# A hybrid decoder step: the sample stage's first loads in another order and on another queue

## The reference

```python
def mixer_block(h, pos, past, w_in, b_gate, w_conv, b_conv, mh_norm_g, w_out):
    proj = jnp.einsum('btd,dc->btc', h, w_in)              # q, k, v | raw q/k, v, o, gates of the mLSTM
    ...
    att = dilated_attention_sample(qa, kc, vc)             # 3 patterns: window 128 / 512 step 4 / 2048 step 16
    ...
    hb, C1, n1, m1 = mlstm_chunkwise(qb, kb, vb, ig, lf, C0, n0, m0, chunk)
    hb = hb * lax.rsqrt(jnp.mean(hb * hb, axis=-1, keepdims=True) + EPS)
    hb = hb * mh_norm_g.reshape(MLSTM_HEADS, MLSTM_HD)
    hb = hb * jax.nn.sigmoid(ob.reshape(B, T, MLSTM_HEADS, MLSTM_HD))
    mix = jnp.concatenate([att.reshape(B, T, ATT_WIDTH), hb.reshape(B, T, MLSTM_WIDTH)], axis=-1)
    return jnp.einsum('btc,cd->btd', mix, w_out), ...

hp = hp + a_p; hs = hs + a_s
hp = hp + sqrelu_mlp(rms_norm(hp, norm2_g), w_up, w_down)  # same for hs, then a last rms_norm
```

## Time and profile before

| | before |
|---|---|
| median of 3 runs | 2995.48 us (2992.3 to 2998.82) |
| the profiled execution | 2989.5 us, its span 2987.7 us |
| busy share of the span: TensorE, weight loads, VectorE, ScalarE, POOL | 96, 83, 48, 31, 34% |
| mean granted TensorE clock | 0.984 |

### The profile page before, as it was taken

One profiled execution on the slowest core, in us unless ns is written; L12 is line 12 of the kernel. 1 busy time (PEld: TensorE's weight loads), 2 busy tenths in 40 slices (PEclk: granted clock), 3 DMA queues, 4 the chain that ended last, 5 costly groups with the idle time before them and its releaser, 6 DMA issues.

```text
span 2987.7 us, 47542 instructions
## 1 busy us (share of the span) xinstructions
PE 2855.3 (96%) x18291; PEld 2478.0 (83%) x18291; DVE 1427.7 (48%) x3363; ACT 926.2 (31%) x1741; POOL 1003.3 (34%) x590
## 2 busy tenths in 40 slices
PE   7999999998999968899999999999999999999997
PEld 5878788887777756678799999989999998899996
DVE  5522555334888845586343333344333333544444
ACT  4301322112767742332132221243212222422222
POOL 1212012211455530210064343444434344545443
PEclk8999999999999988999999999999999999999999
DMA  4322223334464448955352323235222323533332
GB/s 137 113 102 97 97 94 122 106 117 147 133 193 155 160 141 335 370 174 187 134 220 94 126 93 107 94 122 225 94 108 93 126 93 117 207 129 131 138 126 83
DMA packets 124794, 421.41 MB, mean 141 GB/s; under 512 B 18655, under 2 KB 44387, under 8 KB 104918
## 3 DMA queue, kind: packets, MB, share of 16 engines
q1 hardware_dynamic: 103836, 366.53, 34.7%
q10 hardware_dynamic: 19658, 48.68, 4.2%
q0 software_dynamic: 1152, 4.19, 0.5%
HBM read 350.83 MB, written 135.63 MB: 163 GB/s over the span
## 4 chain that ended last, share of the span: by engine, by line
PE 48%; ACT 1%; POOL 1%; DVE 0%; DMA 0%; issue 0%; ACTq 0%
PE mlp_bank L220 16%; PE mlp_bank L221 16%; PE mlp_bank L222 16%; PE mlp_bank L236 0%; PE mlp_bank L235 0%; POOL mlp_wu_lo L2634 0%; DMA mlp_xb<-x 0%; PE mlp_bank L2982 0%; DVE mlp_acc L2854 0%; POOL mlp_xb L2676 0%; ACT mlp_wu_hi L2692 0%; ACT mlp_acc L2767 0%; DVE mlp_hT_lo L2903 0%; DVE mlp_acc L2871 0%; POOL mlp_acc L2681 0%
## 5 line engine op out<-in xcount | busy, mean ns | idle before, releaser
L2854 DVE TENSOR_TENSOR mlp_acc<-mlp_acc,mlp_bank 128x512 f32<-128x512 f32 x542 | 348.2, 684 | 365.7 <-PE mlp_bank L222 357.6
L220 PE MATMUL mlp_bank<-mlp_hT_hi,mlp_wu_hi 128*128 128x384 f32 (+1 forms) x1536 | 496.0, 323 | 3.1 <-PEq L3122 3.1
L222 PE MATMUL mlp_bank<-mlp_hT_hi,mlp_wu_lo 128*128 128x384 f32 (+1 forms) x1536 | 494.6, 322 | 0.0
L221 PE MATMUL mlp_bank<-mlp_hT_lo,mlp_wu_hi 128*128 128x384 f32 (+1 forms) x1536 | 494.4, 322 | 0.0
L2842 DVE TENSOR_TENSOR mlp_xn<-mlp_xn 128x384 f32<-128x384 f32 (+1 forms) x192 | 203.8, 1068 | 509.5 <-ACT mlp_xn L2710 489.3
L220 PE MATMUL mlp_bank<-mlp_wd_hi,mlp_u_hi 128*128 128x512 f32 x1024 | 400.0, 391 | 5.0 <-DVE mlp_acc L2854 5.0
L221 PE MATMUL mlp_bank<-mlp_wd_lo,mlp_u_hi 128*128 128x512 f32 x1024 | 398.9, 390 | 0.0
L222 PE MATMUL mlp_bank<-mlp_wd_hi,mlp_u_lo 128*128 128x512 f32 x1024 | 398.8, 389 | 0.0
L2638 POOL TENSOR_TENSOR mlp_wd_lo<-mlp_wd_raw,mlp_wd_hi 128x2048 fp32r<-128x2048 f32 x48 | 221.8, 4621 | 391.6 <-ACT mlp_wd_hi L2698 391.6
L2647 POOL TENSOR_TENSOR mlp_u_lo<-mlp_xn,mlp_u_hi 128x384 fp32r<-128x384 f32 (+1 forms) x192 | 177.9, 938 | 359.0 <-ACT mlp_u_hi L2719 359.0
L220 PEld LDWEIGHTS mlp_bank<-mlp_hT_hi,mlp_wu_hi 128*128 128x128 f32 x1536 | 288.2, 188 | 5.2 <-issue 3.5
(11 more groups left out here) (370 smaller groups left out, 4693.6 us busy)
## 6 DMA issues: line engine op xcount, KB each, us to landing
mlp_wu_raw<-in_w_up SPq DMA_DIRECT2D x48, 1024.0 KB, 4.9
mlp_wd_raw<-in_w_down SPq DMA_DIRECT2D x48, 1024.0 KB, 4.9
out_win_k_sample<-in_cache_k SPq DMA_DIRECT2D x48, 680.0 KB, 6.3
out_win_v_sample<-in_cache_v SPq DMA_DIRECT2D x48, 680.0 KB, 7.2
p_w_raw<-in_w_tok SPq DMA_DIRECT2D x10, 2048.0 KB
sm_vin<-in_cache_v SPq DMA_DIRECT2D x8, 2048.0 KB, 12.3
proj<-p_stage ACTq DMA_DIRECT2D x53, 256.0 KB, 2.0
parts<-mx_part SPq DMA_DIRECT2D x48, 264.0 KB, 3.9
```

What stands on the lines that cost most here:

```text
L220: nc.tensor.matmul(out, ah, bh, start=(k == 0), stop=False)
L221: nc.tensor.matmul(out, ah, bl, start=False, stop=False)
L222: ins = nc.tensor.matmul(out, al, bh, start=False, stop=(k == n - 1))
L2854: ins = v.tensor_tensor(acc[:, t, 512 * e:512 * e + 512], acc[:, t, 512 * e:512 * e + 512], bank[4 + 2 * (t % 2) + e][:], ALU.add)
```

## The change

Four edits:

1. `mix_prompt`'s SP no longer waits at its end until its last stores (`part_out`, `hb_out`) have landed. The semaphores live on into `mix_sample`, where SP waits for the same counts behind `load_k(1)`.
2. SP in `mix_sample` issues `load_k(1)` first, then the tables `mask` and `mask_new`, `vnew` and the first two value windows.
3. The nine small loads (arg x 4, maskS, vx, seq1, obs, mhg) are issued by ScalarE on its own queue, ahead of its first computation.
4. `mask` and `mask_new` lie behind `pr` and `qz` in the region `front`, ahead of them before.

```diff
 # mix_prompt
-        part_out = [[sem(f"mx_part_out{a}{p}") for p in range(2)] for a in range(3)]
-        hb_out = [sem(f"mx_hb_out{p}") for p in range(2)]
+        part_out, hb_out = K.part_out, K.hb_out
...
             sp.wait_ge(s["next_in"], 16 * (2 + SAMPLE_ROWS))
-            for a in range(3):
-                for p in range(2):
-                    sp.wait_ge(part_out[a][p], 16 * (NCH // 2))
-            for p in range(2):
-                sp.wait_ge(hb_out[p], 16 * (NCH // 2))
 # mix_sample: places
-        mask, mask_new, pr = front("mask", OLD), front("mask_new", DEC_B, NS), front("pr", 2, KEYS)
+        pr = front("pr", 2, KEYS)
...
         qz = front("qz", DEC_B, PAIRS, QW)
+        mask, mask_new = front("mask", OLD), front("mask_new", DEC_B, NS)
 # mix_sample, SP
-            x = s["ml_in"]
+            load_k(1)
+            for a in range(3):
+                for p in range(2):
+                    sp.wait_ge(K.part_out[a][p], 16 * (NCH // 2))
+            for p in range(2):
+                sp.wait_ge(K.hb_out[p], 16 * (NCH // 2))
             sp.dma_start(mask[:], K.ins["sample_mask"]).then_inc(s["tab_in"], 16)
             sp.dma_start(mask_new[:], K.ins["sample_mask_new"]).then_inc(s["tab_in"], 16)
-            for h in range(MH):
-                sp.dma_start(arg[:, h].rearrange("p (b t) -> p b t", b=DEC_B),
-                             K.ng_sample.rearrange("(b h) t -> h b t", h=MH)[h].partition_broadcast(NS)).then_inc(s["arg_in"], 16)
-            sp.dma_start(maskS[:], K.ins["chunk_mask"]).then_inc(s["arg_in"], 16)
-            sp.dma_start(vx[:, :, 0:MD], K.proj[VB, S0:S0 + NS, :].rearrange("p (h d) -> p h d", h=MH)).then_inc(x, 16)
-            sp.dma_start(seq1[:], K.ins["token_seq"]).then_inc(x, 16)
-            sp.dma_start(obs[:], K.proj[OB, S0:S0 + NS, :]).then_inc(x, 16)
-            sp.dma_start(mhg[:], K.ins["mh_norm_g"].partition_broadcast(NS)).then_inc(x, 16)
-            load_k(1)
             sp.dma_start(vnew[:], K.proj[VK, S0:S0 + NS, :]).then_inc(s["vnew_in"], 16)
 # mix_sample, ScalarE
             nc.scalar.preload_act_table_set(LN_EXP)
             own = Chain(act, s["act_ml"])
+            x = s["ml_in"]
+            for h in range(MH):
+                act.dma_start(arg[:, h].rearrange("p (b t) -> p b t", b=DEC_B),
+                              K.ng_sample.rearrange("(b h) t -> h b t", h=MH)[h].partition_broadcast(NS)).then_inc(s["arg_in"], 16)
+            act.dma_start(maskS[:], K.ins["chunk_mask"]).then_inc(s["arg_in"], 16)
+            act.dma_start(vx[:, :, 0:MD], K.proj[VB, S0:S0 + NS, :].rearrange("p (h d) -> p h d", h=MH)).then_inc(x, 16)
+            act.dma_start(seq1[:], K.ins["token_seq"]).then_inc(x, 16)
+            act.dma_start(obs[:], K.proj[OB, S0:S0 + NS, :]).then_inc(x, 16)
+            act.dma_start(mhg[:], K.ins["mh_norm_g"].partition_broadcast(NS)).then_inc(x, 16)
 # mixers
+        K.part_out = [[K.sem(f"mx_part_out{a}{p}") for p in range(2)] for a in range(3)]
+        K.hb_out = [K.sem(f"mx_hb_out{p}") for p in range(2)]
```

## The result

The changed kernel takes 3018.47 us (median of 4 runs, 3014.14 to 3022.59), the kernel before 2995.22 us in runs on the same chip (4 runs). The ratio is 1.0078, with a 95% interval of 1.0066 to 1.0089. The prediction was 2998 with a range of 2990 to 3014. The time lies above it, at the value of the rival "ScalarE is stuck" (3018), to which I gave a chance of 0.12.

The account below looks back on a forecast made before the run. It saw two possible limits, TensorE's waits and late transfers. Start of sm_kin's transposes moving from 1120.96 to 1123.5 gave +2.5 us: profiled 2989.5 becomes 2992.0, and with the runs' median 6.0 above, 2998; range 2990 to 3014.

Parts of the forecast that it names:

- ScalarE is stuck: Rival: sm_arg's records take turns one for one with SP's, holding ScalarE's issues until SP's backlog ends; +22 us, 3018; chance 0.12.
- The stage's earlier start: Sample stage's start: moving SP's 1.0 us wait for mixer stores behind load_k(1) brings the first DMA from 1091.49 to about 1090.5.
- No TensorE wait on sm_kin: Second cached key window, issued first on SP, lands by T0+10, so TensorE's wait of 6.1 us for it goes.
- The tables behind sm_kin: Mask tables queue behind the keys on SP, so VectorE's first key copy comes at T0+16.9 (1107.4), 8.9 us later than before.
- T0: The sample stage's first DMA issue, in each trace its own; forecast at about 1090.5 us.
- The small loads on ScalarE: Nine issues ahead of ScalarE's first work cost 9.9 us, hidden by the mask wait; several small packets pass in a turn.
- ScalarE's start: ScalarE's first work in the sample stage, at 1094.54 before, comes at T0+9.9 = 1100.4 at the earliest.
- The forecast's own end: Last small load, sm_mhg, lands at T0+31 = 1121.5; sm_kin's transposes then start at 1123.5 against 1120.96, +2.5 us.
- the waits just go: Rival: waits at the stage start, for sm_kin and for mhg vanish, 8.7 us faster, 2986.8; needs masks at 1098.5; chance 0.05.
- The clock: Rival: TensorE's slow-clock stretch (0.53, 1158 to 1176) moves, giving back up to 8 us; net faster by over 0.2%: chance 0.08.

Follow-up runs that it names:

- e4: Kernel before with only the mixer-store waits moved and the mask tables placed behind pr and qz; load order and queues as before: 2995.06 us, ratio 0.9996.
- e1: Changed kernel with the nine small loads back on SP's queue, behind the two mask tables, keys still first: 2998.95 us, ratio 1.0009.
- e3: Changed kernel with sm_arg's four loads made one load of 64 rows of 1 KB, small loads still on ScalarE's queue: 2998.26 us, ratio 1.0010.
- e6: Changed kernel with sm_arg as one load and all small loads on SP, between the mask tables and the keys: 2987.26 us, ratio 0.9979.
- e8: e3 with the two mask tables ahead of load_k(1) on SP, small loads on ScalarE's queue: 2987.10 us, ratio 0.9974.
- e9: Changed kernel with only sm_arg's four loads moved to SP, ahead of the keys; the other five stay on ScalarE: 3004.29 us, ratio 1.0029.
- e2: Changed kernel with the mask tables issued ahead of the keys on SP again, small loads still on ScalarE's queue: 3019.84 us in one run.

## Why the prediction was wrong

- **The stage's earlier start: right.** From the issue of C_prompt to the stage's first DMA it is 1.62 us where it was 2.96, so 1.34 us against the 1.0 that was forecast. e4, with this edit and the tables' place alone, has 1.88, a gain of 1.08.
- **No TensorE wait on sm_kin: right**, but only since everything else came later than sm_kin.
- **The tables behind sm_kin: right.** VectorE's first copy was forecast at T0+16.9. In e1, where nothing hides it, it is at T0+17.8, and in e3, which keeps the small loads on ScalarE's queue, at T0+19.8. Its price by itself was forecast as +2.5 us together with sm_mhg, and e1 and e3 measured +3.3 and +2.6. In the changed kernel it is hidden behind ScalarE.
- **The small loads on ScalarE: the step that failed.** The prediction said "One for one isn't what rows show for 32-byte packets" and took "several small ones pass in a turn". The changed kernel's queues show one for one with 32-byte records, over 27 us. The step rested on the earlier trace rows, 0.3 us of trace in which SP's queue passed 57 against POOL's 24. In the same stretch POOL's packets were just coming up: the queue view of before has 32 of them from 1100 to 1101 us, 77 in the next microsecond, 84 in the one after. DMA engines without a POOL packet could pass sm_arg's records freely, and that might explain the 57. But the earlier trace rows itself has POOL's packets at 98.6% of the engines' time, which leaves few such engines, so the 57 stay unexplained. That the turns were one for one in the changed kernel is measured.
- **Hence ScalarE's start.** It was forecast at T0+9.9 at the earliest, "hidden by the wait for the mask (1107.4)". It was T0+36.2. The nine issues were costed by what they had taken on SP ahead of all large loads, 9.9 us. The condition for that price, an empty queue, was gone. The rival "ScalarE is stuck" had the chain right: held until SP's backlog is gone (T0+32.3 forecast, about T0+36 measured), first work at T0+34, sm_kin's transposes at 1143.3 with T0 at 1090.5, which is T0+52.8. Measured: T0+54.5. The backlog took longer since the stretch from 1100 to 1131 moved 347 GB/s and not 428. ScalarE's small records are not the reason: with SP's large rows and them alone the rate was 423 (below), with the state's 4 KB rows beside them 353 and 315 (1100 to 1106 and 1106 to 1112), and 157 when the large rows had ended (1127 to 1131).

```profile
1118.00:1124.00 6.00, 0.00 (x0) 0.00 (x0) 0.00 (x0) 0.00 (x0) 0.00 (x0) 0.50 1.02 423
```

- **The forecast's own end, sm_mhg at T0+31**: it came after T0+36, but was no longer what anyone waited for.
- **The rival "the waits just go" (2986.8)** needed the tables in time. e6 and e8 put the tables first and take the records away, and reach 2987.26 and 2987.10. That is 6.7 and 6.8 us below the kernel before on their chip, where the rival had 8.7, and each keeps a wait (sm_kin 3.0, sm_mhg 8.4) that the rival had gone.
- **The clock** is not part of the story. In the 55 us from the start of sm_kin's transposes TensorE was granted 0.82 before (1120.96 to 1176) and 0.81 in the changed kernel (1146 to 1201). The longer stretch at 0.50 ahead of it (1088.3 to 1132.7) is one in which TensorE had next to nothing to do, and its first transposes, which began at 0.50 in both kernels, took about as long (5.58 and 5.28 us).

The chance for the rival "ScalarE is stuck" was too low for what the rows showed: two stalls of 3.8 and 4.0 us in the earlier trace rows and a count of one for one over 3 us in the earlier trace rows stood against one count over 0.3 us.

Open: where e9's further 5.6 us come from, what ends a hold (e2 shows that it is not one number of records), and the 57 in the earlier trace rows.

## What to carry to other kernels

Before a DMA moves to a computing engine's queue, count its records for each DMA engine, not its bytes: with large loads on another queue, each record costs up to one of their turns, and the computing engine may stand in the issue until many of them have passed. A load of few, long records (here 4 for 128, with the sorting done by the engine that adds anyway) repaired 20 of 23 us with nothing moved. And when several loads are late at once, look for the one that the others hide: repairing the tables alone gained nothing, both repairs together gave 30 us (+23.3 to -6.8).

## What was not expected of the hardware

- Three queues took turns record by record with 32 bytes, 4 KB and up to 16 KB on them: 207, 208 and 207 packets in 6 us.
- The issue of a DMA can hold its engine long: 12.6 us in the fourth load of sm_arg, 16.60 us in sm_maskS. SP with 10.6 MB in large records was not held in the changed kernel; with sm_arg behind sm_kin and the tables it was, 13.33 us (e1). So it is not the bytes that count. Fewer and longer records for the same 64 KB ended the holds (e3). But no fixed number of outstanding records fits: holds ended with an estimated 77 and 72 left on each DMA engine in the changed kernel and 53 in e2, and e2's fourth load went out unheld with 99 ahead of it.
